# Two pairs of heads per score step on four quarters of the TensorE array, and bias sum and row extreme in one VectorE instruction

## The reference, cut to what matters

```python
scores = jnp.einsum('bhrnqd,bhrnikd->bhrnqik', q_blk, kg)      # q already times 64 ** -0.5
scores = scores + bias[None]                                    # rpb by relative row and column, per head
scores = jnp.where(valid[:, :, None, :], scores, -1e30)
probs = jax.nn.softmax(scores, axis=(-2, -1)).astype(v.dtype)
out = jnp.einsum('bhrnqik,bhrnikd->bhrnqd', probs, vg)
```

## Time and profile before

| | |
|---|---|
| median of three runs | 3776.81 us |
| the profiled execution, its span | 3778.2 us |
| TensorE busy in the span | 95% |
| the attention of the first block (first score to first matmul of the next stage) | 167.4 to 324.6 us |
| TensorE busy from 165 to 325 us | 143.5 of 160 us |

### The profile page before, as it was taken

One profiled execution on the slowest core, in us unless ns is written; L12 is line 12 of the kernel. 1 busy time (PEld: TensorE's weight loads), 2 busy tenths in 40 slices (PEclk: granted clock), 3 DMA queues, 4 the chain that ended last, 5 costly groups with the idle time before them and its releaser, 6 DMA issues. The chain is left out here.

```text
span 3778.2 us, 46616 instructions
## 1 busy us (share of the span) xinstructions
PE 3606.1 (95%) x18410; PEld 2808.8 (74%) x18410; DVE 1848.7 (49%) x3350; ACT 1185.7 (31%) x2093; POOL 702.7 (19%) x532
## 2 busy tenths in 40 slices
PE   7999999999999999999988988988999999999998
PEld 6756778888888888876557878646788468888886
DVE  4276992223685554244468884469321142232322
ACT  3155771222311211132434553128311032211210
POOL 1162000010101111010020110119201213333333
PEclk9999999999999999998998996999999999999999
DMA  3100111112233222113011212200122111111111
GB/s 131 38 2 25 42 39 56 53 56 78 89 95 109 92 90 95 51 60 123 1 22 33 46 34 72 78 17 2 26 73 64 56 54 47 45 56 45 45 56 45
DMA packets 266342, 211.67 MB, mean 56 GB/s; under 512 B 65680, under 2 KB 231184, under 8 KB 265744
## 3 DMA queue, kind: packets, MB, share of 16 engines
q1 hardware_dynamic: 264368, 201.61, 17.3%
q10 hardware_dynamic: 1760, 7.08, 0.9%
HBM read 185.33 MB, written 21.50 MB: 55 GB/s over the span
## 5 line engine op out<-in xcount | busy, mean ns | idle before, releaser
L95 PE MATMUL ps<-halves 128*128 128x512 f32 x10408 | 2408.2, 392 | 18.8 <-DVE halves L1542 6.6
L95 PEld LDWEIGHTS ps<-halves 128*128 128x128 f32 x10408 | 1957.1, 188 | 441.4 <-issue 26.9
L95 PE MATMUL ps<-arena 128*128 128x512 f32 (+2 forms) x1040 | 397.1, 540 | 11.6 <-issue 6.0
L95 PEld LDWEIGHTS ps<-arena 128*128 128x128 f32 x1040 | 199.4, 213 | 172.4 <-issue 160.3
L1521 POOL TENSOR_TENSOR tmps<-tmps 128x512 f32<-128x512 f32 x128 | 143.5, 1121 | 981.4 <-ACT tmps L1489 981.4
L1542 DVE TENSOR_TENSOR halves<-tmps,halves 128x512 fp32r<-128x512 f32 x128 | 89.0, 698 | 433.4 <-ACT halves L1497 433.4
L1425 ACT ACTIVATE halves<-raws 128x2048 fp32r<-128x2048 f32 x62 | 118.4, 1910 | 554.7 <-PE ps L95 532.5
L1528 POOL TENSOR_TENSOR arena<-arena 128x512 f32<-128x512 f32 x128 | 164.7, 1294 | 191.4 <-DVE arena L1569 191.4
L1489 ACT ACTIVATE tmps<-ps 128x512 f32<-128x512 f32 x128 | 76.6, 598 | 364.0 <-PE ps L95 354.0
L1569 DVE TENSOR_TENSOR arena<-ps,arena 128x512 f32<-128x512 f32 x128 | 87.7, 690 | 194.6 <-PE ps L95 188.5
L1365 DVE SCALAR_TENSOR_TENSOR arena<-arena,sc 128x128 f32<-128x128 f32 x448 | 163.4, 365 | 15.9
(11 more groups left out here) (300 smaller groups left out, 3548.7 us busy)
## 6 DMA issues: line engine op xcount, KB each, us to landing
raws<-in_w_ff SPq DMA_DIRECT2D x31, 1024.0 KB, 6.5
raws<-in_w_mlp SPq DMA_DIRECT2D x31, 1024.0 KB, 5.3
mixw<-in_w_in SPq DMA_DIRECT2D x56, 512.0 KB, 4.0
arena<-in_w_ada SPq DMA_DIRECT2D x48, 512.0 KB, 3.9
arena<-in_w_in SPq DMA_DIRECT2D x5, 2048.0 KB, 8.8
arena<-in_x SPq DMA_DIRECT2D x8, 1024.0 KB, 8.2
h_stash<-arena SPq DMA_DIRECT2D x1, 5120.0 KB, 20.6
inverses<-arena ACTq DMA_DIRECT2D x20, 256.0 KB, 2.9
```

The lines of the kernel that those rows point to most:

```text
L95: ins = e.matmul(out_ap, l, r, start=i == 0, stop=i == n - 1)
```

## The change

- The scores of two units, i and i + 1 with i even, are issued together: four matmuls of 64 rows by 64 columns of weights, each with 512 moving columns. Head s of a pair lies in rows 64 s to 64 s + 63 of the array; unit i puts head s on columns and partitions 64 s, the odd unit i + 1 puts it on the other half (`natt_rows`). So the four matmuls take the four quarters of the array, and two banks, each bank written by a pair of diagonal quarters. No multiplication by zeros is left. The issue order is: head 0 of unit i, head 0 of unit i + 1, head 1 of unit i, head 1 of unit i + 1.
- Six banks are opened in two iterations as before, now in the order scores(i), scores(i + 1), transposes(i - 3), values(i - 4), transposes(i - 2), values(i - 3). Scores wait for both banks. Scores' emptying has a counter of its own.
- Bias sum and extreme are one `tensor_tensor_reduce`: it writes -(scores + bias) to `sb` and the row's minimum of that to `statn`. The exp takes `sb` with scale -1. The wait between the two instructions goes.
- VectorE's order over two iterations is now: sum(i), output(i - 4), sum(i + 1), reciprocal(i), output(i - 3), reciprocal(i + 1), for i even.
- `QB` needs no zeros, so the two memsets go, and a bank of queries is taken out by one instruction of 128 partitions. It waits until all eight token tiles of the first norm are scaled, since `QB` lies on `X`.
- The bias is laid out with the heads of odd pairs exchanged; the values' matmuls take the columns by `natt_rows`.

```diff
         def vector_query_out(e, m, h):
             key = ("q", m, h)
-            e.wait_ge(*q_zero.at(m // 2 + 1))
+            e.wait_ge(*n_xn.at(8))
             e.wait_ge(*bk.full(key))
-            for s in range(2):
-                rows = slice(64 * s, 64 * s + 64)
-                ins = e.tensor_scalar(
-                    QB[rows, m, 8 * h:8 * h + 8, s, :],
-                    bk.tile(key)[rows, :].rearrange("p (r q) -> p r q", q=64), V("bq", m)[rows], 0.125,
-                    ALU.add, ALU.mult)
-            ins.then_inc(*bk.emptying(key))
+            e.tensor_scalar(QB[:, m, 8 * h:8 * h + 8, 0, :], bk.tile(key)[:, :].rearrange("p (r q) -> p r q", q=64),
+                            V("bq", m), 0.125, ALU.add, ALU.mult).then_inc(*bk.emptying(key))
...
         def gpsimd_qkv(e):
-            for i in range(2):
-                e.wait_ge(*n_xn.at(4 * i + 4))
-                e.memset(R(F0 + 4096 * i, 4096), 0.0).then_inc(*q_zero.tick())
...
+        def natt_rows(i, s):
+
+            a = 64 * ((s + i) % 2)
+            return slice(a, a + 64)
+
         def tensor_natt(e):
             for i in range(64 + 4):
-                if i < 64:
-                    r, j, start = natt_place(i)
-                    key = ("as", i)
-                    o = bk.open(key, a_ev)
-                    e.wait_ge(*bk.vacant(key))
+                if i < 64 and i % 2 == 0:
+                    for u in (i, i + 1):
+                        bk.open(("as", u), a_es)
+                        e.wait_ge(*bk.vacant(("as", u)))
...
-                    e.matmul(o[:, :], QB[:, j, r, :, :], KT[:, j, start * 64:start * 64 + 512], start=True,
-                             stop=True).then_inc(*bk.filling(key))
+                    for s in range(2):
+                        for u in (i, i + 1):
+                            r, j, start = natt_place(u)
+                            f = slice(64 * s, 64 * s + 64)
+                            ins = e.matmul(bk.tile(("as", u))[natt_rows(u, s), :], QB[f, j, r, 0, :],
+                                           KT[f, j, start * 64:start * 64 + 512], start=True, stop=True)
+                            if s == 1:
+                                ins.then_inc(*bk.filling(("as", u)))
...
-                    e.tensor_tensor(sb[i % 2], bk.tile(key)[:, :], BI[:, j, off * 64:off * 64 + 512],
-                                    ALU.add).then_inc(*bk.emptying(key))
-                    c = statn[:, i % 8, :]
-                    e.wait_ge(*bk.clear(key))
-                    e.tensor_reduce(c[:, 0:1], sb[i % 2], AX.X, ALU.max, negate=True).then_inc(*a_mx.tick())
-                u = i - 1
-                if 0 <= u < 64:
-                    c = statn[:, u % 8, :]
-                    e.wait_ge(*a_ex.at(u + 1))
-                    e.reciprocal(c[:, 2:3], c[:, 1:2]).then_inc(*a_rc.tick())
-                if 0 <= i - 4 < 64:
...
+                    e.tensor_tensor_reduce(out=sb[i % 2], in0=bk.tile(key)[:, :], in1=BI[:, j, off * 64:off * 64 + 512],
+                                           scale=-1.0, scalar=3.0e38, op0=ALU.add, op1=ALU.min,
+                                           accum_out=statn[:, i % 8, 0:1]).then_inc(*bk.emptying(key))
+                for u in ((), (i - 1, i))[i % 2]:
+                    if u < 64:
+                        c = statn[:, u % 8, :]
+                        if u == i and i >= 4:
+                            vector_natt_out(e, i - 4)
+                        e.wait_ge(*a_ex.at(u + 1))
+                        e.reciprocal(c[:, 2:3], c[:, 1:2]).then_inc(*a_rc.tick())
+                if i >= 4 and (i % 2 == 0 or i >= 64):
+                    vector_natt_out(e, i - 4)
...
         def scalar_natt(e):
             for i in range(64 + 3):
                 if i < 64:
                     c = statn[:, i % 8, :]
-                    e.wait_ge(*a_mx.at(i + 1))
+                    e.wait_ge(*bk.clear(("as", i)))
                     if i >= 5:
                         e.wait_ge(*bk.full(("at", i - 5)))
-                    e.activation(pbuf[i % 5], sb[i % 2], ACT.Exp, bias=c[:, 0:1],
+                    e.activation(pbuf[i % 5], sb[i % 2], ACT.Exp, bias=c[:, 0:1], scale=-1.0,
                                  accum_out=c[:, 1:2]).then_inc(*a_ex.tick())
```

More of the change, by code:

```diff
@@ L396, in build @@
         bvr = R(47168, 512)
-        q_zero, q_bias = C("queries_zeroed"), C("bias_masked")
+        q_bias = C("bias_masked")
         p_ev, p_ea = C("qkv_emptied_dve"), C("qkv_emptied_act")
@@ L573, in build @@
         statn = sm[:, 8:32].rearrange("p (a b) -> p a b", b=3)
-        a_ev, a_ea = C("natt_emptied_dve"), C("natt_emptied_act")
-        a_mx, a_ex, a_rc, a_sl = C("natt_max"), C("natt_exp"), C("natt_recip"), C("natt_scaled")
+        a_es, a_ev, a_ea = C("natt_emptied_scores"), C("natt_emptied_values"), C("natt_emptied_act")
+        a_ex, a_rc, a_sl = C("natt_exp"), C("natt_recip"), C("natt_scaled")
         def natt_place(i):
@@ L617, in tensor_natt @@
                             ins = e.matmul(o[f, 0:64], vals[:, start // 2 + c, j * 128 + 64 * s:j * 128 + 64 * s + 64],
-                                           ptb[u % 3][:, c, f], start=c == 0, stop=c == 3)
+                                           ptb[u % 3][:, c, natt_rows(u, s)], start=c == 0, stop=c == 3)
                     ins.then_inc(*bk.filling(key))
@@ new lines, in vector_natt, with vector_natt_out @@
+                for u in ((), (i - 1, i))[i % 2]:
[7 more added lines that the diff above has]
+                    vector_natt_out(e, i - 4)
+        def vector_natt_out(e, u):
+            r, j, start = natt_place(u)
+            key = ("ap", u)
+            e.wait_ge(*bk.full(key))
+            e.tensor_copy(YAH[:, j, r, :], bk.tile(key)[:, 0:64]).then_inc(*dv.tick())
+            e.wait_ge(*dv.now())
+            e.tensor_tensor(YAL[:, j, r, :], bk.tile(key)[:, 0:64], YAH[:, j, r, :].bitcast(F32),
+                            ALU.subtract).then_inc(*bk.emptying(key))
@@ L3285, in layout @@
     nb = a["rpb"][0][:, :, idx]
-    nb = nb.reshape(4, 2, 15, 64, 64).transpose(1, 3, 0, 2, 4)
+    nb = nb.reshape(4, 2, 15, 64, 64)
+    nb = np.stack([nb[j, ::-1] if j % 2 else nb[j] for j in range(4)]).transpose(1, 3, 0, 2, 4)
     got["nbias"] = np.ascontiguousarray(nb.reshape(128, 4, 960))
```

## The result

The changed kernel took 3743.27 us, the median of five runs (3738.40, 3741.87, 3743.27, 3753.70, 3755.63), beside 3767.11 us for the kernel before in the same series (five runs, 3763.57 to 3777.61; the three of the section on the time before are among them). The ratio is 0.9932, with a 95% interval of 0.9912 to 0.9953. The kernel is faster, by 24 us between these medians and by 18 to 33 us according to the interval. Forecast were 3757.0 us and a range from 3748 to 3776: the sign and the mechanism came out, the absolute time lies 13.7 us under the forecast and 4.7 us under the range.

What follows compares the result with a forecast made beforehand. A chain of waits across engines, 4.67 us per two units, was taken to bound the attention. From the profiled 3778.2 us, 19.3 (attention) and 0.5 (queries) gave 3758.4, less 1.4 to the median: 3757.0 us, range 3748 to 3776.

Steps and rivals of the forecast that it cites:

- What bounds it: Attention: no engine full; a chain from scores to the scores two units later, 4.67 us for two units, bounds it.
- Accumulator added: Joined bias sum and minimum on VectorE: adds 0.10 us to the sum alone, bounds 0 and 0.69.
- the first rival: Joined VectorE instruction is slow, at the scan's rate: only 4.2 us gained, 3772.6 us; chance 0.13.
- Scores: Attention scores on TensorE: four quarters work at once, a pair holds it 0.97 us and takes 1.12.
- the rival with two quarters: Scores on TensorE: only two quarters work at once, 1.94 us for 0.97, 3785.6 us; chance 0.08.
- New chain: Attention: scores, sum, exp, copy, values to next scores takes 4.05 us a pair, 2.025 a unit.
- the rival of the clock: TensorE, less busy in the attention, falls to 1.2 GHz in more stretches; ten of them give 3772 us; chance 0.04.
- Start: Start of the attention: units 0 to 5 gain nothing, shifted values' landing doesn't move, exp(6) starts at about 184.5 us.
- End: End of the attention: from exp(63) to the next stage stays 5.4 us.
- Queries: Query banks lose one 0.75 us instruction each; only the one before the splits counts, gain 0.5 us, bounds 0 and 0.76.
- Memsets: Memsets on GpSimd: nobody waits for them, so removing them gains nothing.
- Sum: Whole kernel: profiled 3778.2 less 19.3 and 0.5 gives 3758.4, which is 1.4 above the median: 3757.0 us.

Runs made afterwards that it cites:

- two quarters: Changed kernel with both units of a pair on the same two diagonal quarters, issued head by head; single run 3759.57 us, attention 153.5 us.
- quarters alone: Changed kernel with bias sum and maximum as two VectorE instructions again, scores still on four quarters; 3769.17 us, ratio 0.9982 to the kernel before.
- after, again: Changed kernel run again without any edit, six runs; 3744.22 us, ratio 0.9923 to the kernel before.
- joined instruction alone: Kernel before with only bias sum and maximum joined into one VectorE instruction; 3761.62 us, ratio 0.9968 to the kernel before.
- two quarters, unit by unit: Changed kernel with both units on the same two diagonal quarters, both heads of unit i issued before unit i + 1's; single run 3757.35 us.
- bias sums later: Changed kernel with GpSimd's four mask-to-bias additions held until all eight token tiles are scaled; single run 3735.82 us.
- scores ahead: Changed kernel with the next pair's scores issued one iteration earlier, behind the even iteration's values; 3738.59 us, ratio 0.9906 to the kernel before.
- both: Changed kernel with the next pair's scores issued earlier and GpSimd's bias additions held back, six runs; 3737.44 us, ratio 0.9903 to the kernel before.

## Why the prediction was right or wrong

**What bounds it** held. The chain, its links and its order were read rightly from the earlier trace rows, and the stage behind the attention handed the gain on: the stretch behind it is as long as before, 1258.4 us for 1257.1, and as full.

**Maximum gone:** right, 0.72 us a pair.

**Accumulator added,** forecast 0.10, bounds 0 and 0.69: it came out at the lower end. The instruction takes 685 ns, the read behind it 83 ns; by starts it is 0.73 us from the joined instruction to the exp, where it was 0.72 from the sum to the maximum. The added cost is 0.01 us. The forecast counted a read of 0.15 us whose overlap was only guessed; the read starts 0.62 us after the instruction does, so it lies inside its tail. The scan's rate, the first rival, is excluded.

**Scores,** 0.97 hold and 1.12 long: measured 1.02 from the scores' start to that of the transposes behind them, and 1.09 long. Scores to sum took 1.14, not 1.17. Right, and the rival with two quarters, rebuilt, costs 1.94. The Trainium skill ("TensorEngine Tiling (Array Packing)", "Restrictions and Gotchas", PSUM pressure) says that different row tiles can't access one PSUM bank simultaneously. Here the four MATMULs of both row halves start within 0.02 us, and each bank takes one of each half, on its own partitions. The measurement decides, and the rule doesn't hold for this form.

**New chain,** 4.05 us a pair: 3.93. The difference, 0.12, is the 0.09 of the accumulator and the 0.03 of the scores. From exp(6) to exp(63) it was 1.959 a unit for 2.025, so 57 x 0.066 = 3.8 us more gain than forecast. The order on VectorE cost nothing, as said. The granted clock from 165 to 325 us was 0.97 for 0.99: the rival of the clock shows at the start alone, where it was 0.74 from 165 to 185 us (0.91 before).

**Start,** exp(6) at 184.5 less the 0.5 of the queries: 183.60, 0.4 us more gain. Two things there were not forecast and were covered: until 173.12 us TensorE waited 4.20 us for GpSimd (before, 2.64), and it ran the second pair's scores at the 1.2 GHz level (1.99 us for 1.09). The wait for the shifted values shrank from 3.29 to 1.43 us in their place. The landing moved with the earlier start, from 179.29 to 178.59.

**End,** 5.4 us: 300.65 - 295.25 = 5.40. **Queries:** the wait in the earlier trace rows went from 3.58 to 3.12 us, 0.46 for the 0.5 taken. **Memsets:** "nothing" was right for the time as far as TensorE's wait shows it, but not for what happens: what GpSimd does next moved ahead by 12 us, onto VectorE's scalings.

**Sum.** 19.8 us forecast, and 0.4 + 3.8 more: 24.0 in the profile. Alone, the joined instruction gave 12.7 us and the quarters 1.6; both together gave 23.3 from the first exp on (153.6 - 130.35). The excess over their sum, 9 us, is that each alone runs into what the other removes: the joined instruction into TensorE's 2.11 us a unit, the quarters into the chain.

**The step that failed** is the last one, from the gain to the absolute time and its range. The forecast, 3757.0, is the median of three runs, 3776.81, less the gain of 19.8. With the gain as measured, 24.0, it would have been 3752.8, inside the range; so 4.2 of the 13.7 us are the gain, and 9.5 are this base and its scatter. In the series of the result the same kernel before had 3767.11 as its median, 9.7 us under the base. That is no sign that the base was unusual: the 34 later runs of the kernel before have a median of 3775.5, but they reach from 3762.49 to 3783.88, and medians of a few of them move by 10 us. As a measure of scatter the prediction took only the lowest of three runs. It also added up wrongly: 3757.0 less 2.85 (no accumulator cost) less 9.7 (3776.81 - 3767.11) is 3744.5 and not 3748, and even that lies 1.2 us above the result. With the lowest of the 34 runs in place of the lowest of three, the same sum gives 3739.8.

One smaller term was wrong without effect. The span of 3778.2 us was set 1.4 above the median; the profiles taken since show 1.8 us outside the span (3738.4 for a span of 3736.6), so that this execution took about 3780, an estimate. The forecast took the 1.4 off again.

What the scatter is made of was followed through the profiles. The middle stretch, of some 950 us, beside the mean granted clock of the execution:

| profile | attention | middle stretch | mean granted clock |
|---|---|---|---|
| before | 153.6 | 960.6 | 0.972 |
| quarters alone | 152.0 | 946.5 | 0.975 |
| after | 130.35 | 941.8 | 0.976 |
| after, again | 130.5 | 938.7 | 0.977 |
| joined instruction alone | 140.9 | 950.5 | 0.975 |
| two quarters | 153.5 | 941.5 | 0.977 |
| two quarters, unit by unit | 139.3 | 955.4 | 0.973 |
| bias sums later | 129.0 | 941.8 | 0.976 |
| scores ahead | 117.4 | 960.7 | 0.971 |
| both | 116.4 | 956.0 | 0.971 |

The middle stretch goes with the clock and not with the attention: two quarters have the attention of before, and a middle stretch 19 us shorter. So in before against after the 18.8 us are no effect of the change that I can show.

The runs say the same. A straight line through the 34 runs of before, time against mean clock (given to 0.001), falls by 2.7 us for each 0.001 and leaves 2.2 us of scatter. Under this line the joined instruction alone lies 12.3 us (ten runs), the quarters alone 5.2 (ten), the changed kernel 26.6 (eleven), the scores ahead, with those of "both", 39.7 (twelve). Part of it is the attention's own clock: 0.97 for 0.99 over 160 us takes 0.0009 off the mean, which the line counts as some 2 us; without it 26.6 comes near the 24 of the profile. And the scores ahead are 13.1 us faster than the changed kernel at an equal clock, as much as the attention says. Only 6 of them show in the medians, because these twelve runs had a mean clock of 0.9714 and the eleven of the changed kernel 0.9735, beside 0.9728 for the 34 of before; 0.0021 are 5.6 us on the line. Why their clock was lower stays open. Either it is chance, or work that comes earlier by 13 us lets more of the middle stretch fall to the 1.2 GHz level. No run separates the two.

## What to carry to other kernels

Read the chain by starts and ask of each saved microsecond whether it is a link: the quarters alone halved a step and gave 1.6 us, the joined instruction alone removed a link and gave 12.7, and both 23.3, because the first lifts the bound that the second runs into. Where several banks are filled in one block, the chain sees when the first is reported full: with two quarters the order of issue alone was worth 14 us, where packing four quarters in place of two was worth 23. Before a forecast in absolute time, put the spread of the kernel's own runs into the range, since a gain of 24 us was measured on top of a scatter of 21. And compare runs at an equal mean clock: this brought out 13 us of which the medians showed 6.

## What the runs showed of the hardware that I had not expected

- Issue order does not bind the starts in different quarters of the array, but the signals kept to it: with two matmuls for one quarter issued before those for the other, the eight MATMULs still took 1.94 us, four rounds and not seven. Unit i's last MATMUL started in the second round, at 241.31 us, and was signalled behind the fourth, at 242.77.
- A sum with running minimum over 512 f32 elements takes no longer than the sum alone (685 ns for 691), and its accumulator's read, 83 ns, hides in its tail.
- VectorE's scaling of 1024 f32 elements takes 0.75 us (four in 2.74, since they overlap). One that starts beside an addition of GpSimd with two inputs took 2.2 to 2.7 us in the profiles. In that of after only the first of the four lies beside one and takes 2.26; in the changed kernel's second profile the first two do, and they take 2.25 and 2.74:

```profile
23.84 9.35 POOL L556 TENSOR_TENSOR arena<-arena 128x960 f32<-128x960 f32 x4 [23.42 <-DMA arena<-in_rows]
...
28.83 6.23 DVE L327 TENSOR_SCALAR arena<-arena,sm 128x1024 f32<-128x1024 f32 x4
```

Each of these scalings ends some 0.55 us behind the end of the addition beside which it started (33.13 for 32.58 us in the profile of after; 31.08 for 30.52 and 33.74 for 33.18 in the second). That is the picture of an instruction that waits for the other engine's to end, more than of two that share; it is read off, not tested. Even a scaling of 4 elements (line 308) took 2.01 us instead of 0.17 beside an addition. GpSimd's four additions take 8.88 us with no scaling beside them (bias sums later) and 9.35 here, of which the last has 2.70 for 2.25. The Trainium skill ("GPSIMD Engine Reference", "Specifications") says that GpSimd's SBUF interfaces are shared with VectorE, with contention against VectorE's two-port modes or two SBUF inputs. The rows agree that there is contention, and give it a size: up to 3.7 times for one of VectorE's scalings. They have one input, and no run shows in which mode they ran.
